# Evaluating all 16384 experts of the last block with matrix products from streamed tables, in place of gathering each token's 128 rows

## The chip, the cores and the metric

One core of a Trainium2 chip runs the whole program. A core has five engines that run side by side and meet only at semaphores: TensorE (matmul), VectorE, ScalarE, GpSimd, and SyncE, which here only issues DMAs. The metric is device microseconds of one execution, the median of the runs.

## The reference, cut to what matters

256 tokens of width 1024 pass two blocks (gated recurrence, latent attention, memory attention) and a last block of another kind: modulated norm, dilated attention beside a pooling mixer, and then a feed-forward part that picks experts. All is float32. The last part, for h = the normed and modulated tokens:

```
q = (h @ w_q).reshape(C, 8, 2, 128)                 # 8 retrieval heads, 2 halves
s = einsum('chpk,pnk->chpn', q, sub_keys)           # 128 sub-keys per half
sv, si = top_k(s, 16)
cand = sv[:,:,0,:,None] + sv[:,:,1,None,:]          # 256 candidates a head
top_v, top_pos = top_k(cand, 16)
eid = take(si0 * 128 + si1, top_pos)                # 16384 experts
gate = softmax(top_v)
act = gelu(einsum('cd,chkd->chk', h, expert_u[eid]))
y = einsum('chk,chkd->cd', gate * act, expert_v[eid])
out = rmsnorm(x + g2 * y, final_g)
```

Every token picks 8 x 16 = 128 of 16384 experts; an expert is one row of 1024 in each of two tables of 64 MB.

## The kernel before, in words

The program is unrolled. An order of tasks is written out for each engine and each of the three blocks: PE_ORDER, ACT_ORDER and ACT_LAST, DVE_ORDER and DVE_LAST; every engine works through its list strictly in order, and waits on semaphores inside a task. Tokens are two tiles of 128 (`t` and `u` in the names of tasks: K0at is unit K0, first half of its columns, tile 0). Weights come through `ring`, three slots of 2 MB, issued by SyncE; a slot is loaded again when TensorE has counted `unit_done`. Unit K2 alone goes to two other tiles (`aside`).

In the last block TensorE makes, after attention, the output product (tasks O1, O0), the transposes of the normed tokens into `xT` (Zt, Zu), the expert queries (K0 to K3, `expert_queries`) and the scores against the sub-keys (E0t to E3t, EU0, EU1, E4 to E7). VectorE turns scores into picks: `route(t, e)` is one top-16 search of a head and tile (tasks Rt0 to Rt7, Ru0 to Ru7), `experts_of` with `centre` finds the expert's numbers of a part of a tile (XP1 to XP7), and `gates_of` (GT) makes the gates, behind an exponential on ScalarE (T). OM, NM and Zu on VectorE are the residual sum, the norm and half of the scaling of the transposed tokens.

The picks are then gathered: for each of 256 pairs (tile, pick) GpSimd issues an indirect DMA (L626) that brings for each of 128 tokens a row of 8 KB, u and v of its expert side by side, into one of 15 slots. VectorE makes the dot product with the token (`dots_of`, L1841), ScalarE its gelu, times the gate, spread over a diagonal of 128x128 (`expert_weights`, L1305 to L1313), and TensorE sums diagonal x v rows into PSUM (L1087, tasks W). A slot is free again after that. The first gather is issued as soon as one head of tile 0 is known (XP1). At the end `end_sums` and `finish` add to x, norm and scale (FS, FN).

Before that, GpSimd multiplies the modulation matrix (L590 to L593) and mixes the pool. PSUM has two double tiles `pj` for units and outputs, and four banks that take turns (`bank_index`); from Zt on only two turn, since the others hold the sums. `do(...)` waits for its own instruction before the next one of the engine is issued.

Of the kernel before, what the change touches and what calls it, by code (L numbers as in the profile page):

```python
# [10 lines left out]


# [26 lines left out]
ROWS = PICKS * TT  # L39
GROUP = 4  # L40
N_SLOTS = 15
N_DIAG = 8
# [24 lines left out]
            Y5 O1u Zt O0v K0at E0t O0w K0bt E1t K1at Zu K1bt E2t K0au W4 K0bu E3t W5 W7 EU0 K1au W11 K1bu W15 EU1 W21  # L67
            K20 W27 K21 W31 K22 W32 K23 W36 E4 W37 E5 W40 K30 W42 K31 W45 K32 W49 K33 W55 E6 E7 W256"""]
# [4 lines left out]
ACT_LAST = """Xu BU BK BQa BQb SK S0 S1 MT S2 BV P0 P1 S3 S4 P2 S5 P3 P4 P5 OMt Zt K0at E0t T1 K0bt E1t OMu Zu K1bt W1  # L73
    E2t W5 E3t W7 K0bu W8 T2 W11 EU0 W18 K1bu W20 T3 W21 EU1 W35 K23 W38 E4 W39 E5 W51 T4 W57 K33 W61 E6 W62
    E7 W65 T5 W96 T6 W129 T7 W148 FN0 W256 FN1"""
# [4 lines left out]
DVE_LAST = """Xu S0 S1 S2 PL0 PL1 N0 N1 S3 N2 S4 S5 N3 N4 Y1 N5 OMt Y5 NMt Zt Rt0 XP1 OMu H2t NMu D1 Zu D3 H2u D4 GT1  # L80
    D5 Rt1 D8 XP2 D9 Rt2 D15 Rt3 D16 GT2 D18 XP3 D37 GT3 D44 Rt4 D50 Rt5 D54 XP4 D62 GT4 D63 Rt6 Rt7 D72 XP5
    D77 GT5 Ru0 D81 Ru1 D83 Ru2 Ru3 D89 XP6 D104 GT6 D105 Ru4 D106 Ru5 D110 Ru6 D115 Ru7 D121 XP7 D137 GT7
    D140 FS0 D156 FN0 D256 FS1 FN1"""


def pe_tasks():

    out, loads, pieces = [], 0, 0
    for text in PE_ORDER:
        tasks = []  # L90
        for task in text.split():
            if task == "LD":
                task, loads = f"LD{loads}", loads + 1
            if task == "AD":
                task, pieces = f"AD{pieces}", pieces + 1
            tasks.append(task)
        out.append(tasks)
    assert loads == pieces == N_MOD_PIECES
    return out
# [46 lines left out]
def big_uses():  # L146

    out, uses, turn = {}, [0, 0], 0
    for l, name in STREAM:
# [4 lines left out]
        elif name in ONE_SLOT or name == "C":  # L154
            if name in ("K1", "K2", "K3"):
                turn = 1
            out[l, name] = (turn, uses[turn])
            uses[turn] += 1
            turn = 1 - turn
    return out  # L160


BIG = big_uses()
# [12 lines left out]
def bank_uses(l, task):  # L176
# [7 lines left out]
    if task[0] == "E":  # L184
        return [(task,)]
# [21 lines left out]
EXPERT_PARTS = [(0, 0, 1), (0, 1, 2), (0, 2, 4), (0, 4, 6), (0, 6, 8), (1, 0, 4), (1, 4, 8)]  # L207


def part_starts():  # L210

    return {tile * PICKS + first * TOPK: n + 1 for n, (tile, first, last) in enumerate(EXPERT_PARTS)}


def bank_index():

    out, n, uses = {}, 0, [0, 0, 0, 0]

    def use(key, at):
        out[key] = (n, at, uses[at])  # L220
        uses[at] += 1
    for l in range(DEPTH + 1):
        few = False
        for task in TASKS[l]:
            few = few or (l == B2 and task == "Zt")
            for key in bank_uses(l, task):
                use((l, key), n % 2 if few else n % 4)
                n += 1
    return out, uses


def picks_order():

    free, out, last = [], [], {}
    for n in range(ROWS):
        if n in NEW_SLOTS:
            free = list(NEW_SLOTS[n][1]) + free
        k = free.pop(0)
        out.append((k, last.get(k), sum(1 for q in out if q[0] == k)))
        last[k] = n  # L240
        free.append(k)
    return out


NEW_SLOTS = {0: ("", range(0, 7)), 18: ("K1", (7, 8)), 41: ("K2", (9, 10)), 67: ("K3", (11, 12, 13)), 74: ("E7", (14,))}


def constants():
# [18 lines left out]
    for d in (4, 16):  # L267
# [14 lines left out]
        "c_iota": np.arange(16, dtype=np.float32).reshape(1, 16),  # L282
# [3 lines left out]
def build(nc, d, out):  # L286
# [8 lines left out]
    BANK, BANK_USES = bank_index()  # L295
    PICK = picks_order()

    with ExitStack() as ctx:
        def sb(name, shape, dt=f32):
            return ctx.enter_context(nc.sbuf_tensor(name, shape, dt))  # L300


# [8 lines left out]
        more_rows = sb("more_rows", [P, 2, D_MODEL])  # L311
# [4 lines left out]
        rope = sb("rope", [P, 2, T])  # L316
# [16 lines left out]
        qM = sb("qM", [P, MLA_HEADS, T])
        kM = sb("kM", [P, MLA_HEADS, T])
        vM = sb("vM", [P, TT, MLA_HEADS * MLA_V])
        qvE = sb("qvE", [P, 2, MEM_HEADS * T])
        qE = qvE[:, 0, :].rearrange("p (h t) -> p h t", t=T)
        kE = sb("kE", [P, MEM_HEADS, T])
        vE = qvE[:, 1, :].rearrange("p (a n) -> p a n", a=TT)
        sm = sb("sm", [P, 2, TT, T])  # L340
        pT = sb("pT", [P, 2, TT, T])
# [10 lines left out]
        w_pool, iota = flat_pair[:, 0:4 * P].rearrange("p (h t) -> p h t", t=P), mod_part[:, 1, 0:TOPK]  # L352
        sub_rows = flat_pair[:, 528:528 + 2 * P]
        row_gate1, row_scale2 = hv[:, 0, :], hv[:, 1, :]
        row_shift2, row_gate2, final_g = big[:, 0, :], big[:, 1, :], big[:, 2, :]
# [15 lines left out]
        def flat(tile):  # L371
# [15 lines left out]
        id_a, id_b = flat(vM)[:, 2 * PICKS:3 * PICKS], flat(vM)[:, 3 * PICKS:4 * PICKS]  # L387
        expert = flat(vM)[:, 512:768].bitcast(u32).rearrange("p (t j) -> p t j", t=TT)
        dots = flat(vM)[:, 768:1024].rearrange("p (t j) -> p t j", t=TT)
        onehot = flat(qT).rearrange("p (j i) -> p j i", i=TOPK)  # L390

        ring_rows = [[ring[:, UNIT[B2, unit] % RING, g * 2 * D_MODEL:(g + 1) * 2 * D_MODEL] for g in range(2)]
                     for unit in ("K1", "K2", "K3")]
        flat_y = flat(yT)
        aside = [flat(b), flat_y[:, 2 * D_MODEL:]]
        row_slot = ([flat(more_rows), flat(kM), flat(qvE), flat(qM)] + ring_rows[1] + [flat(hv)]
                    + ring_rows[0] + aside + ring_rows[2] + [flat(xT), flat_y[:, 0:2 * D_MODEL]])
        assert len(row_slot) == N_SLOTS
        diag = [far_pair[:, g, :] for g in range(4)] + [causal[:, g // 2, (g % 2) * P:(g % 2 + 1) * P] for g in range(4)]
        assert len(diag) == N_DIAG  # L400
        junk = [flat_pair, big[:, 0, :]]
        acts, weights_of = rope[:, 0, :], rope[:, 1, :]
        first_scores = [sm[:, i // 2, i % 2, :] for i in range(4)] + [pT[:, i // 2, i % 2, :] for i in range(4)]
        later_scores = kT
        pj = [ctx.enter_context(nc.psum_tensor(f"pj{i}", [P, 1024], f32)) for i in range(2)]
# [46 lines left out]
        SCORES_OF = {name: n for n, name in enumerate(t for t in ACT_LAST.split() if t[0] == "E")}  # L452
# [29 lines left out]
        N_B2 = 5  # L482
# [5 lines left out]
        def _(sp):  # L488
# [5 lines left out]
            def weights(n):  # L494

                if STREAM[n] == (B2, "K2"):
                    sp.wait_ge(sem("pool_out"), 2)
                    for g in range(2):
                        load(aside[g], d["units"][n, :, g * 2 * D_MODEL:(g + 1) * 2 * D_MODEL], "aside_load")
                    return  # L500
# [31 lines left out]
            for l in range(DEPTH + 1):  # L532
                units = [name for k, name in LOADS if k == l]
                for name in units:
# [14 lines left out]
                    if UNIT[l, name] > 1 and name != "K2":  # L549
                        weights(UNIT[l, name])  # L550
                    if name == "K0":
                        weights(UNIT[l, "K2"])
                    if name == units[3] and l == B2:
# [4 lines left out]
                        for row, c in ((row_gate1, 2), (row_scale2, 4), (row_shift2, 3), (row_gate2, 5)):  # L558
                            load(row, mod_rows[c * DC:(c + 1) * DC, :].rearrange("(o c) p -> o (c p)", o=1)
# [1454 lines left out]
```

## Time and profile before

| | |
|---|---|
| time, median of 3 runs | 1456.43 us (1456.28 to 1457.4) |
| span of the profiled execution | 1455.4 us |
| TensorE busy | 1312.6 us (90%) |
| VectorE busy | 815.5 us (56%) |
| GpSimd busy | 647.9 us (45%) |
| ScalarE busy | 412.4 us (28%) |
| moved by DMA | 407.7 MB, mean 280 GB/s |

The shares of busy time are means over parts with different limits, so they must be read by stretch. Matmuls are pipelined, and a busy TensorE is not one at its peak.

### The profile page before, as it was taken

What the parts mean: (1) busy time and instruction counts of PE and PEld (TensorE: products, weight loads), DVE (VectorE), ACT (ScalarE), POOL (GpSimd) and SP (SyncE); (2) the same over time, 40 slices, a digit from 0 to 9 for tenths busy, and PEclk for the clock granted to TensorE, in tenths of its full rate; (3) what the DMA queues carried; (4) which work ended last, traced back from release to release, by engine and by line L of the source; (5) the groups of instructions that cost most, each with busy time, mean ns of one, the idle gap of its engine ahead of it and who ended that gap; (6) DMA issues with size and microseconds to landing.
All of it is one profiled execution on the core that took longest, in us unless ns stands there. A gap on an engine that the chain in (4) does not pass through costs nothing.

```text
span 1455.4 us, 14776 instructions
## 1 busy us (share of the span) xinstructions
PE 1312.6 (90%) x4936; PEld 829.2 (57%) x4936; DVE 815.5 (56%) x1680; ACT 412.4 (28%) x1032; POOL 647.9 (45%) x643
## 2 busy tenths in 40 slices
PE   9999999999999999999998989967877787778886
PEld 8888687747888687747656646533333332323332
DVE  0775377431465367443237775879887654544555
ACT  0532244211332244112232332322313232122123
POOL 0556667331546667331202434454544454544440
PEclk9999999999999999999999999988989899999999
DMA  9544334345443334357255999999999999999995
GB/s 375 189 160 174 116 152 172 133 184 199 187 161 158 132 143 176 116 202 257 69 231 232 377 413 409 421 420 419 420 419 421 419 420 420 420 420 420 420 420 211
DMA packets 53734, 407.71 MB, mean 280 GB/s; under 512 B 6150, under 2 KB 8731, under 8 KB 11035
## 3 DMA queue, kind: packets, MB, share of 16 engines
q0 software_dynamic: 36864, 268.45, 44.7%
q1 hardware_dynamic: 15706, 137.28, 24.2%
q10 hardware_dynamic: 1088, 1.05, 0.4%
q8 instruction: 39, 0.64, 0.2%
q14 instruction: 37, 0.30, 0.1%
HBM read 404.63 MB, written 1.07 MB: 279 GB/s over the span
## 4 chain that ended last, share of the span: by engine, by line
PE 63%; DMA 23%; DVE 7%; issue 3%; ACT 2%; POOL 1%; ACTq 0%; POOLq 0%; DVEq 0%
PE pj L665 23%; DMA ring<-in_peer_uv,vM 10%; PE bank L1087 10%; PE pj L701 9%; PE pj L680 7%; DMA yT<-in_peer_uv,vM 5%; PE bank L805 3%; DMA more_rows<-in_peer_uv,vM 3%; DMA qvE<-in_peer_uv,vM 2%; PE pj L957 2%; DMA hv<-in_peer_uv,vM 2%; DMA qM<-in_peer_uv,vM 1%; PE bank L638 1%; PE bank L907 1%; DVE tri L1841 1%
## 5 line engine op out<-in xcount | busy, mean ns | idle before, releaser
L665 PE MATMUL pj<-xT,ring 128*128 128x256 f32 (+2 forms) x1536 | 324.3, 371 | 1.8 <-ACTq L1135 1.7
L665 PEld LDWEIGHTS pj<-xT,ring 128*128 128x128 f32 (+1 forms) x1536 | 277.7, 189 | 42.4 <-issue 2.7
L592 POOL TENSOR_SCALAR more_rows<-more_rows,lbt 128x256 f32<-128x256 f32 x168 | 178.4, 1062 | 16.4
L626 POOL DMA_INDIRECT ring<-in_peer_uv,vM x101 | 120.1, 1189 | 116.5 <-PE bank L1087 104.4
L590 POOL TENSOR_SCALAR mod_part<-more_rows,lbt 128x256 f32<-128x256 f32 x24 | 26.1, 1088 | 271.2 <-issue 120.0
L701 PE MATMUL pj<-ring,yT 128*128 128x512 f32 x320 | 140.3, 594 | 0.0
L1305 ACT ACTIVATE rope<-vM 128x4 f32<-128x4 f32 (+3 forms) x84 | 17.1, 204 | 408.0 <-DVE big L1841 325.2
L593 POOL TENSOR_TENSOR mod_part<-mod_part,more_rows 128x256 f32<-128x256 f32 x168 | 126.5, 753 | 14.0
L1087 PE MATMUL bank<-ring,causal 128*128 128x512 f32 x200 | 99.3, 635 | 17.4 <-ACT causal L1313 17.4
L1087 PE MATMUL bank<-ring,tri 128*128 128x512 f32 x204 | 97.6, 618 | 16.5 <-ACT tri L1313 16.5
L701 PEld LDWEIGHTS pj<-ring,yT 128*128 128x128 f32 x320 | 59.9, 190 | 71.1 <-issue 71.1
L1841 DVE SCALAR_TENSOR_TENSOR big<-ring,memT 128x1024 f32<-128x1024 f32 x51 | 62.7, 1230 | 48.3 <-DMA ring<-in_peer_uv,vM 48.1
L1841 DVE SCALAR_TENSOR_TENSOR tri<-ring,memT 128x1024 f32<-128x1024 f32 x50 | 61.3, 1226 | 48.2 <-DMA ring<-in_peer_uv,vM 48.1
L1087 PEld LDWEIGHTS bank<-ring,causal 128*128 128x128 f32 x200 | 39.6, 202 | 70.4 <-issue 45.3
L1087 PEld LDWEIGHTS bank<-ring,tri 128*128 128x128 f32 x204 | 39.8, 199 | 69.5 <-issue 46.4
L626 POOL DMA_INDIRECT more_rows<-in_peer_uv,vM x20 | 21.7, 1087 | 121.9 <-DVE vM L1811 79.4
L680 PE MATMUL pj<-ring,xT 128*128 128x512 f32 x160 | 70.3, 594 | 0.0
L805 PEld LDWEIGHTS bank<-big 128*128 128x128 f32 x480 | 57.4, 192 | 3.9 <-issue 3.2
L805 PE MATMUL bank<-big 128*128 128x128 f32 x480 | 58.4, 275 | 0.0
L1307 ACT ACTIVATE rope<-rope,rstd 128x1 f32<-128x1 f32 x256 | 56.6, 284 | 2.8
L680 PEld LDWEIGHTS pj<-ring,xT 128*128 128x128 f32 x160 | 29.9, 190 | 34.6 <-issue 34.4
L957 PEld LDWEIGHTS pj<-xT,ring 128*128 128x128 f32 x320 | 43.3, 199 | 6.2 <-issue 4.7
(366 smaller groups left out, 2146.3 us busy)
## 6 DMA issues: line engine op xcount, KB each, us to landing
ring<-in_units SPq DMA_DIRECT2D x44, 2048.0 KB, 9.3
more_rows<-in_w_ada SPq DMA_DIRECT2D x24, 1024.0 KB, 4.8
ring<-in_units SPq DMA_DIRECT2D x2, 1536.0 KB, 6.5
ring<-in_peer_uv,vM POOLq DMA_INDIRECT x101, 23.2
memT<-in_mem SPq DMA_DIRECT2D x1, 1024.0 KB, 5.4
ring<-in_units SPq DMA_DIRECT2D x2, 512.0 KB, 6.6
ring<-in_units SPq DMA_DIRECT2D x1, 1024.0 KB, 9.0
xT<-in_x_turned SPq DMA_DIRECT2D x1, 1024.0 KB, 10.8
```

Of the source, the lines that this page charges most:

```text
L590: do(g.tensor_scalar(part, mod_w[:, 0, :], silu_c[:, 0:1], None, ALU.mult))
L592: do(g.tensor_scalar(mod_w[:, c, :], mod_w[:, c, :], silu_c[:, c:c + 1], None, ALU.mult))
L593: do(g.tensor_tensor(part, part, mod_w[:, c, :], ALU.add), "mod_partial" if c == DC - 1 else None)
L626: pool.indirect_dma_start(row_slot[k], None, d["peer_uv_2"], bass.IndirectOffsetOnAxis(ap=expert[:, t, j:j + 1], axis=0))\
L665: ins = nc.tensor.matmul(pj[s][0:n, 2 * m + first:2 * m + stop], ring[:, slot, at:at + n], act[:, c, first:stop], start=(c == 0), stop=(c ...
L680: ins = nc.tensor.matmul(pj[s][:, t * COLS:(t + 1) * COLS], act[:, c, t * P:(t + 1) * P], w[:, c, :], start=(c == 0), stop=(c == DC - 1))
L701: ins = nc.tensor.matmul(pj[t][:, n * 512:(n + 1) * 512], yT[:, 4 * j + c, t * P:(t + 1) * P], w[:, c, n * 512:(n + 1) * 512], start=(firs ...
L805: ins = nc.tensor.matmul(B[:, n * P:(n + 1) * P], k, q, start=True, stop=True)
L957: ins = nc.tensor.matmul(pj[s][:, 2 * m * P + first:2 * m * P + stop], w[c][:, m * P:(m + 1) * P], xT[:, c, first:stop], start=(c == 0), s ...
L1087: ins = nc.tensor.matmul(bank[2 * (1 - t) + half][:, :], diag[n % N_DIAG], row_slot[PICK[n][0]][:, c0:c0 + COLS], start=(j == 0), stop=(j ...
L1307: a.activation(weights_of[:, n0 + k:n0 + k + 1], acts[:, n0 + k:n0 + k + 1], ACT.Copy, scale=gate[:, t, j + k:j + k + 1]).then_inc(sem("ro ...
L1841: v.scalar_tensor_tensor(out=junk[0 if one else n % 2], in0=row_slot[k][:, 0:D_MODEL], scalar=1.0, in1=normed[:, t, :], op0=ALU.mult, op1= ...
```

## The change

In the last block all experts are evaluated for all tokens. `expert_units` lays the two tables out as 64 + 64 pieces of 1 MB, each a pair of first-key values with all 128 second keys (256 experts); SyncE streams them through four half slots of the ring. Task u`p` (of 64) makes u x tokens for pair p, ScalarE's Gelu puts it into `mixture`, 128 second keys x (128 first keys x 256 tokens). The gates are spread over it by one-hot products: for a group of four tokens (tasks g0 to g63) a one-hot of the first keys (`left`, built by GpSimd for three groups of four, else by VectorE) times a one-hot of the second keys scaled by the gates (`right`, VectorE) gives 128 x 128 gates a token, with which VectorE multiplies the columns of `mixture` that are there (`group_weighted`); for pairs that come later ScalarE stores the gates first and VectorE multiplies them by the pair's Gelu (`pair_weighted`). Groups run between pairs 34 and 63. The first keys, second keys and gates of a tile are turned by TensorE before (it0 after u17, it1 after u33). Then tasks v0 to v63 sum mixture x v into `pj`. The gather, the dots, the diagonals and their products go. Expert numbers are no longer put together; the four parts of picks have four heads each. K2 goes through the ring. The banks turn by four throughout. Most tiles of the earlier blocks lie now inside one arena with `mixture`.

```diff
-            Y5 O1u Zt O0v K0at E0t O0w K0bt E1t K1at Zu K1bt E2t K0au W4 K0bu E3t W5 W7 EU0 K1au W11 K1bu W15 EU1 W21
-            K20 W27 K21 W31 K22 W32 K23 W36 E4 W37 E5 W40 K30 W42 K31 W45 K32 W49 K33 W55 E6 E7 W256"""]
+            Y5 O1u Zt O0v K0at O0w K0bt E0t K1at E1t K1bt E2t E3t Zu K0au K0bu K1au EU0 K1bu K20 EU1 K21 K22 K23 K30
+            E4 E5 K31 K32 K33"""]
...
-DVE_LAST = """Xu S0 S1 S2 PL0 PL1 N0 N1 S3 N2 S4 S5 N3 N4 Y1 N5 OMt Y5 NMt Zt Rt0 XP1 OMu H2t NMu D1 Zu D3 H2u D4 GT1
...
+DVE_LAST = """Xu S0 S1 S2 PL0 PL1 N0 N1 S3 N2 S4 S5 N3 N4 Y1 N5 OMt Y5 NMt Zt Rt0 OMu NMu Rt1 Zu Rt2 Rt3 XP1 Rt4
+    Rt5 GT1 Rt6 Rt7 XP2 Ru0 Ru1 GT2 Ru2 Ru3 XP3 Ru4 Ru5 GT3 Ru6 Ru7 XP4 GT4"""
+N_PAIRS = 64
+N_GROUPS = 64
+LEAD = 3
+def expert_tasks():
+
+    out = ["u0", "E6", "E7"]
+    for p in range(1, N_PAIRS):
+        if p > FIRST_MIXED:
+            share = N_GROUPS * (p - FIRST_MIXED) // (N_PAIRS - 1 - FIRST_MIXED)
+            before = N_GROUPS * (p - 1 - FIRST_MIXED) // (N_PAIRS - 1 - FIRST_MIXED)
+            out += [f"g{g}" for g in range(before, share)]
+        out.append(f"u{p}")
+        if p in TURNED_AFTER:
+            out.append(f"it{TURNED_AFTER.index(p)}")
+    return out + [f"v{p}" for p in range(N_PAIRS)]
+TURNED_AFTER = (17, 33)
+FIRST_MIXED = 34
+LEFT_BY_POOL = [g for g in range(N_GROUPS) if g % 4 != 3]
+EXP_AFTER = {1: 1, 9: 2, 21: 3, 31: 4}
...
+            for n in range(2 * N_PAIRS):
+                if n < 4:
+                    unit_done(sp, B2, ("K1", "K1", "K2", "K2")[n])
+                elif n - 4 < N_PAIRS:
+                    bank_filled(sp, (B2, (f"u{n - 4}",)))
+                else:
+                    sp.wait_ge(sem("values_summed"), n - 4 - N_PAIRS + 1)
+                load(pieces[n % 4], d["experts"][n], f"piece_load{n % 4}")
...
+            unit_done(pool, B2, "K3")
+            for g in LEFT_BY_POOL:
+                pool.wait_ge(sem("picks_turned"), 4 * g // P + 1)
+                if g >= LEAD:
+                    bank_filled(pool, (B2, (f"g{g - LEAD}",)))
+                for k in range(4):
+                    t = 4 * g + k
+                    g_left = left[g % LEAD][:, k, :]
+                    nc.gpsimd.tensor_scalar(g_left, iota, first_turned[:, t:t + 1], None, ALU.is_equal)\
+                        .then_inc(sem("left_built"), 1)
...
+                elif task[0] == "u":
+                    p = int(task[1:])
+                    key = (l, (task,))
+                    pe.wait_ge(sem(f"piece_load{p % 4}"), 16 * (p // 4 + 1))
+                    bank_empty(pe, key)
+                    for k in range(2):
+                        for c in range(DC):
+                            at = (k * DC + c) * P
+                            ins = nc.tensor.matmul(bank_of(key)[:, k * T:(k + 1) * T], pieces[p % 4][:, at:at + P],
+                                                   xT[:, c, :], start=(c == 0), stop=(c == DC - 1))
+                    last(ins)
+                elif task[0] == "g":
...
+                    for k in range(4):
+                        ins = nc.tensor.matmul(bank_of(key)[:, k * P:(k + 1) * P], left[g % LEAD][:, k, :],
+                                               right[g % LEAD][:, k, :], start=True, stop=True)
+                    last(ins)
+                elif task[0] == "v" and int(task[1:]) < N_PAIRS - 2:
...
+                    for k in range(2):
+                        for t in range(TT):
+                            for half in range(2):
+                                at = k * D_MODEL + half * COLS
+                                ins = nc.tensor.matmul(pj[t][:, half * COLS:(half + 1) * COLS],
+                                                       mixture[:, 2 * p + k, t * P:(t + 1) * P],
+                                                       pieces[n % 4][:, at:at + COLS],
+                                                       start=(p == 0 and k == 0), stop=False)
+                    last(ins, "values_summed")
...
+                    if known:
+                        turn = p - FIRST_MIXED - 1
+                        if turn >= 2:
+                            act.wait_ge(sem("pair_weighted"), turn - 1)
+                        if known < T:
+                            do(a.activation(mixture[:, e, known:T], B[:, :, known:T], ACT.Gelu))
+                        do(a.activation(hidden_of[p % 2][:, :, 0:known], B[:, :, 0:known], ACT.Gelu), *bank_free(key))
+                    else:
+                        do(a.activation(mixture[:, e, :], B, ACT.Gelu), *bank_free(key))
+                    act.sem_inc(sem("hidden"), 1)
+                    if p in EXP_AFTER:
+                        top_exp(EXP_AFTER[p])
...
+            def right_of(g):
...
+                if g not in LEFT_BY_POOL:
+                    t = 4 * g
+                    v.tensor_tensor(left[g % LEAD], iota.unsqueeze(1).to_broadcast([P, 4, P]),
+                                    first_turned[:, t:t + 4].unsqueeze(2).to_broadcast([P, 4, P]),
+                                    ALU.is_equal).then_inc(sem("left_filled"), 1)
+                for k in range(4):
+                    t = 4 * g + k
+                    v.tensor_scalar(right[g % LEAD][:, k, :], iota, second_turned[:, t:t + 1], gate_turned[:, t:t + 1],
+                                    ALU.is_equal, ALU.mult).then_inc(sem("right_built"), 1)
+
+            def group_weighted(g):
...
+                do(v.tensor_tensor(part, bank_of(key)[:, :].rearrange("p (t e) -> p e t", t=4)[:, 0:e, :], part, ALU.mult),
+                   *bank_free(key))
...
+            def pair_weighted(p):
...
+                do(v.tensor_tensor(part, hidden_of[p % 2][:, :, 0:known], part, ALU.mult), "pair_weighted")
```

## Rows read from the trace of the kernel before

**Rows 1.** The page's slices: clock and DMA in 40 equal parts of the span.
```profile
PEclk9999999999999999999999999988989899999999
DMA  9544334345443334357255999999999999999995
```

**Rows 2.** Busy time by stretch, two stretches; the first line names the columns.
```profile
core 0: us, PE busy (x) PEld busy (x) DVE busy (x) ACT busy (x) POOL busy (x), PEclk, DMA share, GB/s
8.00:35.00 27.00, 27.00 (x126) 22.39 (x125) 0.00 (x0) 1.01 (x1) 0.00 (x0) 1.00 1.00 406
900.00:1400.00 500.00, 397.11 (x891) 174.92 (x890) 329.37 (x778) 131.99 (x481) 240.44 (x204) 0.92 1.01 420
```

**Rows 3.** The page's DMA queues: packets, MB, share of the engines; the gather's queue.
```profile
q0 software_dynamic: 36864, 268.45, 44.7%
```

**Rows 4.** The chain that ended last: start, length in us, what; around 1200 us.
```profile
1184.74 3.46 PE bank L1087 x4
...
1188.46 23.30 DMA ring<-in_peer_uv,vM
```

**Rows 5.** Timeline: start, length in us, engine and line; transposes, one search, OMu, norm.
```profile
761.57 1.04 PE L638 MATMUL bank<-eye,memT 128*128 128x128 f32 x8
...
771.38 0.49 DVE L1754 MAX8 cT<-sm 128x8 f32<-128x128 f32 x2 [6.92 <-ACTq L1413]
...
775.56 0.42 DVE L1782 FIND_INDEX8 kE<-rstd,sq 128x8 uint32<-128x256 f32 x1
...
781.76 0.69 DVE L1926 TENSOR_TENSOR x<-x,tri 128x512 f32<-128x512 f32 x1
...
785.90 0.75 DVE L1533 TENSOR_SCALAR memT<-x,stat 128x1024 f32<-128x1024 f32 x1
```

**Rows 6.** DMA issues: operation, count, KB each, median us from issue to landing.
```profile
more_rows<-in_w_ada SPq DMA_DIRECT2D x24, 1024.0 KB, 4.8
...
yT<-in_units SPq DMA_DIRECT2D x1, 1024.0 KB, 18.7
```

**Rows 7.** The chain that ended last, as above: runs of matmuls of each form.
```profile
113.27 1.78 PE bank L805 x16
115.06 6.91 PE pj L665 x32
...
270.45 13.84 PE pj L701 x32
...
766.04 3.59 PE pj L957 x32
```

**Rows 8.** Timeline of the end: the last four matmuls.
```profile
1445.41 1.98 PE L1087 MATMUL bank<-ring,causal 128*128 128x512 f32 x4 [0.50 <-ACT causal L1313]
```

**Rows 9.** Groups of VectorE from 700 us on, by form: busy us, mean ns of one.
```profile
L1772 DVE TENSOR_TENSOR sq<-cT 128x256 f32<-128x256 f32 x16 | 6.5, 406 | 0.0
L1801 DVE TENSOR_TENSOR qT<-mod_part,vM 128x1024 f32<-128x1024 f32 x4 | 4.7, 1221 | 0.0
...
L1853 DVE TENSOR_TENSOR pT<-bank,big 128x512 f32<-128x512 f32 x4 | 2.8, 690 | 2.3 <-PE bank L1087 2.3
```

**Rows 10.** Groups of ScalarE from 700 us on, the same columns: the table loads.
```profile
L1305 ACT ACT_TABLE_LOAD x8 | 10.3, 1283 | 20.5 <-DVE big L1841 11.7 <-DVE tri L1841 8.6 <-ACT yT L1386 0.2
```

**Rows 11.** Groups of GpSimd; the last row: one line's durations, min/median/max in ns.
```profile
L592 POOL TENSOR_SCALAR more_rows<-more_rows,lbt 128x256 f32<-128x256 f32 x168 | 178.4, 1062 | 16.4
...
L602 POOL COPY b<-kT 128x256 f32<-128x256 f32 x10 | 4.0, 398 | 0.6
...
L597 POOL COPY kT<-kT 128x1024 f32<-128x1024 f32 x1 | 1.0, 1035 | 50.2 <-ACTq L1348 50.2
...
L592 POOL TENSOR_SCALAR more_rows<-more_rows,lbt x168: 924/926/1777, 47.6 to 631.3; 128x256 f32<-128x256 f32 x168
```

**Rows 12.** VectorE's tensor_scalar on two lines: min/median/max in ns.
```profile
L1479 DVE TENSOR_SCALAR sm<-sm x4: 293/294/453, 54.1 to 385.4; 128x256 f32<-128x256 f32 x4
...
L1533 DVE TENSOR_SCALAR memT<-x,stat x4: 752/753/754, 656.1 to 785.9; 128x1024 f32<-128x1024 f32 x4
```

More of the change, by code:

```diff
@@ L13 @@
+import math
 import numpy as np
@@ L72 @@
     Le18 HO2 HN2 HO3 HN3 LN"""
-ACT_LAST = """Xu BU BK BQa BQb SK S0 S1 MT S2 BV P0 P1 S3 S4 P2 S5 P3 P4 P5 OMt Zt K0at E0t T1 K0bt E1t OMu Zu K1bt W1
-    E2t W5 E3t W7 K0bu W8 T2 W11 EU0 W18 K1bu W20 T3 W21 EU1 W35 K23 W38 E4 W39 E5 W51 T4 W57 K33 W61 E6 W62
-    E7 W65 T5 W96 T6 W129 T7 W148 FN0 W256 FN1"""
+ACT_LAST = """Xu BU BK BQa BQb SK S0 S1 MT S2 BV P0 P1 S3 S4 P2 S5 P3 P4 P5 OMt Zt K0at K0bt E0t OMu K1bt E1t E2t E3t Zu
+    K0bu EU0 K1bu EU1 K23 E4 E5 K33"""
 DVE_ORDER = """F0 N FP0 R0 R1 R2 R3 Da01 KR Da02 S0 Db01 P0 Db02 L01 Da03 S1 L02 AD Db03 Da04 F1 AD S2 Da05 L03 Da06
@@ L159, in big_uses @@
             turn = 1 - turn
-    return out
-BIG = big_uses()
+    return out, uses
+BIG, BIG_USES = big_uses()
 N_MLA = 6
@@ L394, in build @@
[L394 to L401, printed above, removed]
@@ L402, in build @@
-        acts, weights_of = rope[:, 0, :], rope[:, 1, :]
         first_scores = [sm[:, i // 2, i % 2, :] for i in range(4)] + [pT[:, i // 2, i % 2, :] for i in range(4)]
         later_scores = kT
+        mixture = arena[:, :].rearrange("p (e t) -> p e t", t=T)
+        piece_at = [(UNIT[B2, unit] % RING, half) for unit in ("K1", "K2") for half in range(2)]
+        pieces = [ring[:, slot, half * 2 * D_MODEL:(half + 1) * 2 * D_MODEL] for slot, half in piece_at]
+        spare = ring[:, UNIT[B2, "K3"] % RING, :]
@@ new lines, in build @@
+        left = [spare[:, k * 512:(k + 1) * 512].rearrange("p (t i) -> p t i", t=4) for k in range(LEAD)]
+        right = [spare[:, 512 * (LEAD + k):512 * (LEAD + k + 1)].rearrange("p (t i) -> p t i", t=4) for k in range(LEAD)]
+        hidden_of = [spare[:, 512 * (2 * LEAD + k):512 * (2 * LEAD + k + 1)].rearrange("p (e t) -> p e t", e=2)
+                     for k in range(2)]
+        row_gate2, final_g = spare[:, 0:D_MODEL], spare[:, D_MODEL:2 * D_MODEL]
+        ends = [spare[:, k * COLS:(k + 1) * COLS] for k in range(4, 6)]
@@ L943, in expert_queries @@
             def expert_queries(name, columns, tiles):
-                if name == "K2":
-                    pe.wait_ge(sem("aside_load"), 32)
-                    w = [rows.rearrange("p (c n) -> p c n", c=DC // 2)[:, c, :] for rows in aside for c in range(DC // 2)]
-                else:
-                    slot = loaded(l, name)
-                    w = [ring[:, slot, c * COLS:(c + 1) * COLS] for c in range(DC)]
+                slot = loaded(l, name)
+                w = [ring[:, slot, c * COLS:(c + 1) * COLS] for c in range(DC)]
                 s, use = BIG[l, name]
@@ L1423, in _ @@
+            log_exp_tables()
+            for t in range(TT):
+                half_norm(t, "x_last", squares)
         @block.vector
@@ L1807, in experts_of @@
                 for k, (op, arg, place, found) in enumerate(half_ids):
-                    do(v.tensor_reduce(found[:, 0:n], ohs[k], X, ALU.add), behind=1 - k)
-                do(v.scalar_tensor_tensor(out=id_a[:, 0:n], in0=id_a[:, 0:n], scalar=float(NKEYS), in1=id_b[:, 0:n],
-                                          op0=ALU.mult, op1=ALU.add))
-                do(v.tensor_copy(expert[:, t, js], id_a[:, 0:n]), "experts")
+                    do(v.tensor_reduce(found, ohs[k], X, ALU.add), behind=1 - k)
             def centre(part):
@@ L1863, in finish @@
                     c = slice(half * COLS, (half + 1) * COLS)
-                    do(v.tensor_scalar(x[:, t, c], pT_of[half], stat[:, 12 + t:13 + t], None, ALU.mult), "result")
-            dots_first = [task[1:] for task in DVE_LAST.split("H2u")[0].split() if task[0] == "D"]
-            SAME_JUNK = max([4] + [int(n) for n in dots_first])
-            used = 0
+                    do(v.tensor_scalar(x[:, t, c], ends[half], stat[:, 12 + t:13 + t], None, ALU.mult), "result")
             for task in DVE_LAST.split():
```

341 lines of the change are left out of this document (166 added, 175 removed).

## The prediction, made before the changed kernel ran

> **What bounds the kernel now.** I read the profile in this order: the page's slices, the busy time and bytes per stretch, the chain that ended last, then rows of single operations. The slices show TensorE's granted clock at or near its upper level (2.4 GHz) and the DMA engines about half used until a little past the middle, then DMA full for everything that follows [rows 1]. From 900 to 1400 us the 16 DMA engines are busy all the time and move 420 GB/s, while TensorE is busy 397 us of 500, VectorE 329 and GpSimd 240 [rows 2]. What they move is the software queue's 268.45 MB, the gathered expert rows: 256 picks x 128 tokens x 8 KB [rows 3]. 268.45 MB at 420 GB/s is 639 us, by far the longest thing after 800 us. The chain of waits says the same: in it a few microseconds of matmuls stand between one landing of over 20 us and the next [rows 4]. So the last 600 us are bound by bytes gathered. The part before 762 us is bound by TensorE, and the change leaves it alone (one table instead of two and three broadcast rows fewer are loaded there, hidden behind matmuls; I take nothing).
>
> **The change, part by part.** It removes the gather, the dot products, the 128x128 diagonals and their 1024 products, and puts in three dense parts on TensorE. I follow TensorE from the transposes of tile 0, which stand at 761.57 us [rows 5], to the end, since every new part passes through it.
>
> *Bytes.* The tables are 16384 x 1024 x 4 B twice, 134.2 MB, half of what was gathered: 320 us at 420 GB/s. Each pair's matmuls below take 3.46 us for a piece of 1.05 MB, which asks for 303 GB/s. At the kernel's start TensorE ran without a gap while DMA moved 406 GB/s [rows 2], so both at once is possible. A piece is issued when the pair four before it is done, so it has three pair times, 10.4 us, to land; a 1 MB load in rows of 8 KB landed in 4.8 us [rows 6]. DMA is then hidden.
>
> *Queries and scores to the first pair.* Half a query unit of one tile is 32 products of 128 columns, 3.59 us [rows 7]. From 761.57: transposes 1.0, O0v 3.5, K0at 3.6, O0w 3.5, K0bt 3.6, score E0t 0.7, that is 777.5. VectorE's first search (Rt0) so starts at 778.0, after the copy; a search takes 4.6 us, from 771.38 to 775.98 in the trace [rows 5]. Then OMu, four operations of 0.69 with gaps, ends at 785.5. The norm of tile 1 ended 786.65 - 782.45 = 4.2 us after OMu [rows 5], of which about 1 us was other VectorE work now removed: 788.7. VectorE now places Rt1 (4.6) ahead of its half of Zu (1.75): 795.1. TensorE meanwhile runs K1at, K1bt and the scores to 788 and has nothing to do until 795; here the order costs it some 6 us. Then K0au, K0bu, K1au, K1bu 14.4; K20 to K33 eight times 1.73 = 13.8; EU0, EU1, E4, E5 about 3.7: the first pair starts at 827.
>
> *Pairs (u).* 64 x 16 = 1024 products of 128x256. Thirty-two of them took 6.91 us with their weight loads hidden, 0.216 each [rows 7]: 221 us. E6, E7 and the two turns of the picks add 2.5.
>
> *Groups (g).* 64 x 4 products of 128 columns at 1.78/16 = 0.111 [rows 7]: 28.5 us.
>
> *Values (v).* 64 x 8 = 512 products of 128x512 at 13.84/32 = 0.4325 [rows 7]: 221.4 us. Since they follow the last pair and piece loads are four ahead, I see no gap at the joint; the weighting of the last group hides under pair 63.
>
> *End.* After the last product VectorE still has the first tile's scaling to finish (its sums became available only 3.4 us earlier), so the second tile's four operations of 0.69 start about 1.2 us late. 1.2 + 2.9 + 1.4 (products with the final gain) + 0.8 (refining) + 1.0 (scaling) + 2.2 (store and close) = 9.5 us. Before, the span ended 8.0 us after its last product at 1447.4 [rows 8].
>
> TensorE's floor: 827 + 221 + 2.5 + 28.5 + 221.4 + 9.5 = 1310 us of span.
>
> *Are the picks there in time?* VectorE has 16 searches of 4.6 and four expert parts of four heads: six operations of 128x1024 at 1.22 [rows 9] and small ones, 9.2. Rt2, Rt3, XP1 end at 813.5; E4 comes at 822.5, Rt4, Rt5 end at 831.7; GT1 waits for the exponential behind pair 1 (838); Rt6, Rt7, XP2, Ru0, Ru1, GT2 end at 867, while TensorE asks for them after pair 17, at 891. Ru2 to Ru5 and XP3 end at 894, GT3 waits for the exponential behind pair 21 (907), Ru6, Ru7, XP4 end at 926, GT4 waits for pair 31 (942), and TensorE asks after pair 33, at 947. So slacks of 24 and 5 us: no cost, though the second is thin. ScalarE's two table loads of 1.28 [rows 10] around each exponential are covered by four banks of 3.46 us.
>
> *Mixed part: the term in doubt.* Groups run between pairs 34 and 63. TensorE needs 29 x 3.46 + 28.5 = 129 us there. In the same time:
> GpSimd builds the left one-hots of 48 groups: 192 scalar comparisons of 128x128. No such operation is in the trace. Its nearest is the 128x256 multiplication, 0.926 median when undisturbed, 1.062 in the mean [rows 11]. Copies of 256 and 1024 cost 0.398 and 1.035, so 0.83 ns an element and 0.186 fixed. If all but 0.186 of the 0.926 grows with the length, 128 columns cost 0.186 + 0.37 = 0.56; if only the copy's slope does, 0.926 - 0.106 = 0.82. The outer ends are 0.56 and, with nothing saved by shortness and the mean's disturbance, 1.06. I take the midpoint 0.69 times 1.062/0.926 = 1.15, thus 0.79, because VectorE will be busier beside it than it was then. Three groups are built ahead, 180 remain: 142 us.
> VectorE: a right one-hot is a tensor_scalar of 128x128; 0.294 at 256 and 0.753 at 1024 [rows 12] give 0.218. Four are 0.87. Weighting a group reads 394 elements in the mean from PSUM (8 x the pairs ahead); 0.406 at 256 and 0.690 at 512 [rows 9] give 0.56. 64 x 1.43 + 16 left one-hots x 0.69 + 29 pairs x 0.41 + gaps 4 = 118 us; with the 15% of disturbance 136. That the access is strided is not in the trace; it may cost nothing or double the 64 x 0.41 us of elements, + 26.
> GpSimd thus sets the pace by a little, with VectorE close behind, and with only three buffers of one-hots two engines at 90% don't overlap perfectly: I add 6 us. 148 in place of 129: + 19.
> The Trainium skill bears on this (GPSIMD Engine Reference, section 3.1): a one-input body costs about 1.03 cycles an element, however simple. The copies' 0.83 ns agree [rows 11]; by it the comparison would lie at the 0.82 end, times 1.15 = 0.94, and the part would be 180 x 0.94 + 6 = 175, + 46 in place of + 19. That result is one of the rivals.
> Its section 8 says GpSimd shares its SBUF interfaces with VectorE when that works with two SBUF inputs or in its two-port mode; by that the four right one-hots would slow GpSimd most, which no row here can single out.
>
> *Sum.* 1310 + 19 = 1329 us of span. The profiled execution has a span of 1455.4 against the median of 1456.43, so 1 us lies around it: 1330 us.
>
> **Rivals.**
> 1. *TensorE alone bounds.* GpSimd's comparison costs 0.56 to 0.65: 180 x 0.65 = 117, under 129. Time 1310 + 1 + a few of coupling = 1313. For it: the short row. Against it: its mean is 15% over its median already with VectorE half busy.
> 2. *The mixed part is much longer.* GpSimd at 0.94 to 1.06, 175 to 197 us, or VectorE with doubled strided access, 118 + 26 = 144, x 1.15 = 166. Time 1357 to 1379. TensorE idles a quarter of such a part, and where it idled a fifth of the time, the granted clock was 0.92 in the mean, so at the lower level (1.2 GHz) for some of it [rows 2], which adds little as it isn't what is waited for.
> 3. *Late pieces: slower than before.* If a piece lands in L, four pieces in flight let a pair pass every L/3. From L = 10.4 us on this is the bound; at L = 13.6 (128 x (4.53 - 3.46) = 137 us) all gain is gone. A 1 MB load in the trace did take 18.7 us [rows 6], which would make 128 x 6.2 = 798 us of the two dense parts, some 1690 us in all. Against it: that load shared the engines with the gather, and 4.8 us is the figure without.
> 4. *The change doesn't do what it says*: the picks come late and TensorE waits before the groups as it now waits for rows. VectorE's second chain has 5 us of slack; 15% on its last 50 us is 8, less 5, and a start of VectorE 10 us later would add as much: 1335 to 1345.
>
> **How the numbers follow.** Forecast (1320 to 1348) 0.47; rival 1 (1305 to 1320) 0.22; rival 2 0.16; rival 4 0.07; rival 3 0.04; an unseen cost of either kind that leaves it still faster 0.04. The range reaches down to rival 1 and up to most of rival 2: 1305 to 1378, which leaves out about 0.12 to 0.2. Slower by over 0.2% are rival 3 beyond L = 13.6 and unseen mechanisms: 0.05. Within 0.2% (3 us, what a measurement of this kernel can tell from no change): 0.01. Faster: 0.94.
>
> **What would show it.** Right: DMA at about 300 GB/s with a busy share near 0.7 from 827 us on; pairs 3.46 us apart at granted clock 1.0; the first pair at 827 and the first value product near 1098; TensorE in the mixed part waiting for GpSimd's one-hots, and none of them in the value part, which takes 221 us. Rival 1: no wait of TensorE in the mixed part. Rival 2: GpSimd's comparison at 0.9 us or more, or VectorE's weighting over 0.8. Rival 3: TensorE waiting for the ring's pieces. Rival 4: TensorE idle before the turn of the picks, released by the VectorE step that makes the gates. The prediction is wrong if the dense products don't hold their 0.216 and 0.4325 beside streaming.

## The result: 1801 us, slower by 24%, and the profile after

The changed kernel takes 1800.97 us (1800.11 to 1802.15) against 1456.36 us before, a ratio of 1.236 (95% interval 1.2345 to 1.238). The prediction said 1330, in 1305 to 1378. Not only the size is wrong but the sign.

The busy time by stretch of the kernel after: the pairs alone, the part where groups are mixed in, and the value part. The columns are those of [rows 2].

```profile
850.00:1090.00 240.00, 240.00 (x1124) 211.46 (x1123) 75.64 (x313) 37.00 (x58) 7.00 (x12) 1.00 0.42 146
1090.00:1348.00 258.00, 258.00 (x1445) 233.96 (x1444) 128.81 (x352) 38.62 (x121) 111.43 (x180) 1.00 0.35 122
1352.00:1790.00 438.00, 438.00 (x1023) 194.06 (x1022) 6.57 (x13) 4.12 (x9) 0.00 (x0) 1.00 0.43 149
```

TensorE is busy in every microsecond of all three, at granted clock 1.00 (2.4 GHz). DMA, which was full and moved 420 GB/s in [rows 2], now moves 122 to 149 GB/s at a busy share of 0.35 to 0.43. The bound has moved from the bytes to TensorE, as intended, but TensorE has more to do than DMA had.

How much more, the groups of the kernel after say (line, shape and count, then busy us and mean ns of one):

```profile
L1096 PE MATMUL bank<-xT,ring 128*128 128x256 f32 x2048 | 447.5, 379 | 0.0
L1128 PE MATMUL pj<-ring,arena 128*128 128x512 f32 x992 | 425.9, 592 | 0.0
...
L1109 PE MATMUL bank<-ring 128*128 128x128 f32 x512 | 61.8, 275 | 0.0
```

The code of L1096 issues 64 x 16 = 1024 products; the trace has 2048 records. L1128 issues 62 x 8 = 496, the trace has 992 (L1142 has the last 16 as 32); L1109 issues 256, the trace 512. Each record lasts what the prediction took for a whole product: 447.5/2048 = 0.218, 425.9/992 = 0.429, 61.8/512 = 0.121. **A float32 product stands in the trace as two matmul records, and the prediction multiplied the number of products in the code by the time of one record.**

The chain that ended last, for the same stretch (start, length, what), is matmuls almost alone:

```profile
859.52 117.42 PE bank L1096 x544
977.27 110.51 PE bank L1096 x512
...
1352.48 425.73 PE pj L1128 x992
1778.21 13.75 PE pj L1142 x32
```

| stretch | predicted | measured |
|---|---|---|
| to the first pair | 827 | 850.7 |
| pairs and groups | 271 | 501.6 |
| values | 221.4 | 439.7 |
| after the last product | 9.5 | 7.5 |
| span | 1329 | 1799.5 |

The measured ones go by the starts 850.7 (first L1096 matmul) and 1352.3 (first L1128 one), and the end at 1778.21 + 13.75 = 1792.0. The sum with two records a product, 2048 x 0.216 + 512 x 0.111 + 2.5 = 502 and 1024 x 0.4325 = 443, gives both dense parts to 1%. Every duration in it was in the trace before [rows 7].

### The profile page after: what moved, and what is told of

It is laid out like the page before. It is cut to its first block, busy times and chain, and to the rows that moved or that the text cites. A ratio compares the mean times of both kernels' runs of the same rounds, so it can differ in the third digit from the quotient of the medians.

```text
span 1799.5 us, 19294 instructions
## 1 busy us (share of the span) xinstructions
PE 1766.4 (98%) x7502; PEld 1267.8 (70%) x7502; DVE 622.3 (35%) x1467; ACT 316.3 (18%) x589; POOL 464.8 (26%) x579
## 4 chain that ended last, share of the span: by engine, by line
PE 97%; DVE 1%; ACT 1%; issue 1%; DMA 0%; ACTq 0%; SPq 0%; DVEq 0%
PE bank L1096 25%; PE pj L1128 24%; PE pj L675 19%; PE pj L711 8%; PE pj L690 5%; PE pj L963 3%; PE bank L1109 3%; PE bank L815 3%; PE bank L648 1%; PE bank L917 1%; PE pj L1142 1%; PE bank L776 1%; PE bank L849 0%; PE bank L831 0%; PE bank L795 0%
## 5 line engine op out<-in xcount | busy, mean ns | idle before, releaser
L1096 PE MATMUL bank<-xT,ring 128*128 128x256 f32 x2048 | 447.5, 379 | 0.0
L1128 PE MATMUL pj<-ring,arena 128*128 128x512 f32 x992 | 425.9, 592 | 0.0
L1096 PEld LDWEIGHTS bank<-xT,ring 128*128 128x128 f32 x2048 | 386.7, 190 | 51.2
L1128 PEld LDWEIGHTS pj<-ring,arena 128*128 128x128 f32 x992 | 188.5, 190 | 236.8 <-issue 236.8
L637 POOL TENSOR_SCALAR ring<-near,causal 128x128 f32<-128x128 f32 x192 | 118.4, 634 | 518.3 <-ACTq L1460 277.5
L613 POOL TENSOR_SCALAR arena<-arena,lbt 128x256 f32<-128x256 f32 x168 | 176.1, 1048 | 16.4
L711 PE MATMUL pj<-ring,arena 128*128 128x512 f32 x320 | 140.3, 594 | 0.0
L614 POOL TENSOR_TENSOR mod_part<-mod_part,arena 128x256 f32<-128x256 f32 x168 | 128.3, 764 | 14.0
L711 PEld LDWEIGHTS pj<-ring,arena 128*128 128x128 f32 x320 | 59.9, 190 | 71.1 <-issue 71.1
L1911 DVE TENSOR_SCALAR ring<-near,causal,mod_part 128x128 f32<-128x128 f32 x256 | 76.6, 362 | 7.2 <-DVE arena L1922 1.8
L963 PE MATMUL pj<-xT,ring 128*128 128x128 f32 (+1 forms) x384 | 61.7, 325 | 12.7 <-issue 7.4
L1109 PEld LDWEIGHTS bank<-ring 128*128 128x128 f32 x512 | 61.7, 192 | 1.5
L1109 PE MATMUL bank<-ring 128*128 128x128 f32 x512 | 61.8, 275 | 0.0
```

The costliest lines, as they stand in the source:

```text
L613: do(g.tensor_scalar(mod_w[:, c, :], mod_w[:, c, :], silu_c[:, c:c + 1], None, ALU.mult))
L614: do(g.tensor_tensor(part, part, mod_w[:, c, :], ALU.add), "mod_partial" if c == DC - 1 else None)
L637: nc.gpsimd.tensor_scalar(g_left, iota, first_turned[:, t:t + 1], None, ALU.is_equal)\
L711: ins = nc.tensor.matmul(pj[t][:, n * 512:(n + 1) * 512], yT[:, 4 * j + c, t * P:(t + 1) * P], w[:, c, n * 512:(n + 1) * 512], start=(firs ...
L963: ins = nc.tensor.matmul(pj[s][:, 2 * m * P + first:2 * m * P + stop], w[c][:, m * P:(m + 1) * P], xT[:, c, first:stop], start=(c == 0), s ...
L1096: ins = nc.tensor.matmul(bank_of(key)[:, k * T:(k + 1) * T], pieces[p % 4][:, at:at + P], xT[:, c, :], start=(c == 0), stop=(c == DC - 1))
```

## The experiments

Theory A: a float32 product takes two records, so TensorE alone sets the time. Theory B: a product takes what was predicted, and streaming stretches it, by late pieces or contention. That 2048 records are there speaks for A; the first two experiments test it from either side. Runs e1, e2 and e4 leave work out or use wrong weights, so they are tests and not kernels to use.

**e1_v_half** sums only the first 128 experts of each pair:

```diff
-                    for k in range(2):
+                    for k in range(1):
                         for t in range(TT):
                             for half in range(2):
                                 at = k * D_MODEL + half * COLS
```

> Leaves out half of the sum over experts: of each pair only the first 128 experts are summed into the output, 256 fewer products of 128x512; everything else is as in the changed kernel, all 128 pieces are still loaded. Theory A (each float32 product stands in the trace as two matmul records of 0.43 us, so it takes 0.865 us, twice what the prediction counted): the value part shrinks by 248 x 0.865 = 214.5 us (pairs 62 and 63 keep theirs), 1801 becomes 1586. Theory B (a product takes 0.43 us as predicted and the value part is stretched by late pieces or by contention with their streaming): the part stays at about 440 us or loses at most 107 us, so 1694 to 1801.

Measured 1589.66 us, 211.3 less than 1800.97. The value products of this kernel:

```profile
L1128 PE MATMUL pj<-ring,arena 128*128 128x512 f32 x496 | 213.0, 592 | 0.0
```

and its value part, columns as in [rows 2]:

```profile
1350.00:1580.00 230.00, 229.79 (x542) 102.65 (x540) 8.05 (x16) 4.74 (x11) 0.00 (x0) 1.00 0.82 285
```

248 products fewer are 496 records and 213 us fewer: 0.86 us each. DMA now moves 285 GB/s and TensorE is still busy 229.8 of 230 us, so the pieces are not late even at nearly twice the rate. This is theory A, 4 us above its 1586.

**e2_stream_once** loads four pieces in all:

```diff
-                load(pieces[n % 4], d["experts"][n], f"piece_load{n % 4}")
+                if n < 4:
+                    load(pieces[n % 4], d["experts"][n], f"piece_load{n % 4}")
...
-                    pe.wait_ge(sem(f"piece_load{p % 4}"), 16 * (p // 4 + 1))
+                    pe.wait_ge(sem(f"piece_load{p % 4}"), 16)
```

> Leaves the streaming out: only the first four pieces are loaded, all pairs use them again, so the products are the same in number and form but most have the wrong weights. Theory A (TensorE's own count of passes): within 3 us of the changed kernel, 1798 to 1804, with DMA near zero in the dense parts. Theory B (streaming stretches the products): towards the predicted 1330, at least 100 us less than 1801.

Measured 1801.11 us, 0.1 more. Busy time by stretch of this kernel, columns as in [rows 2]: DMA moves 1 GB/s or less.

```profile
1200.00:1350.00 150.00, 150.00 (x844) 136.11 (x843) 78.48 (x204) 21.37 (x72) 64.99 (x104) 1.00 0.00 1
1350.00:1580.00 230.00, 230.00 (x545) 103.12 (x544) 0.69 (x1) 1.88 (x2) 0.00 (x0) 1.00 0.00 0
```

Streaming 134 MB costs this kernel nothing; theory B falls. At the pace that the prediction had in mind, about 300 GB/s, the bytes are tested by e4.

**e3_left_all_pool** gives all left one-hots to GpSimd:

```diff
-LEFT_BY_POOL = [g for g in range(N_GROUPS) if g % 4 != 3]
+LEFT_BY_POOL = [g for g in range(N_GROUPS)]
```

> GpSimd builds the left one-hots of all 64 groups instead of 48. It costs 0.634 us each in the changed kernel's trace: 256 x 0.634 = 162 us of GpSimd in a mixed part that TensorE fills for 257 us. Theory A (TensorE bounds the mixed part, with slack of about 95 us for GpSimd): no change, 1799 to 1803. Rival (the prediction's: the builders set the pace of the mixed part): longer by up to 64 x 0.634 = 41 us.

Measured 1800.87 us: no change. In a stretch of its mixed part (columns as in [rows 2]) GpSimd is busy 86 us of 150, in place of 65 in the same stretch of e2, which has the split of the changed kernel, and TensorE all of it:

```profile
1200.00:1350.00 150.00, 150.00 (x843) 136.11 (x843) 74.20 (x195) 21.37 (x72) 85.91 (x140) 1.00 0.35 120
```

The builders don't set the pace at TensorE's true speed.

**e4_both_half** asks what the rest of the prediction was worth: it gives TensorE, in the pairs and in the values, the work that the prediction had counted. The one-hot products of the groups stay as they are, so they still cost twice what was counted. It is e1 and, for the pairs:

```diff
-                        for c in range(DC):
+                        for c in range(DC // 2):
                             at = (k * DC + c) * P
...
-                                                   xT[:, c, :], start=(c == 0), stop=(c == DC - 1))
+                                                   xT[:, c, :], start=(c == 0), stop=(c == DC // 2 - 1))
```

> Leaves out half of the sum over experts and half of the sum over channels in the expert products: 512 fewer products of 128x256 and 248 fewer of 128x512, so TensorE has in both dense parts about what the prediction gave it. Theory A: 1801 - 512 x 0.432 - 248 x 0.865 = 1801 - 221 - 214.5 = 1365 us if TensorE still bounds the mixed part (29 pairs x 3.46 + 64 groups x 0.89 = 157 us there; GpSimd 192 x 0.634 = 122, VectorE about 64 x 1.8 + 30 = 145). If the builders bound it, some 5 to 20 us more, 1370 to 1385. Pieces then have to come at 303 GB/s. Theory B (streaming is the limit): pieces are waited for, above 1450.

Measured 1368.11 us, 3 from theory A's 1365. The mixed part of this kernel and a stretch of its value part:

```profile
970.00:1130.00 160.00, 160.00 (x991) 147.77 (x991) 128.01 (x356) 39.94 (x126) 112.43 (x180) 1.00 0.58 202
...
1200.00:1350.00 150.00, 150.00 (x350) 66.32 (x350) 0.88 (x2) 0.00 (x0) 0.00 (x0) 1.00 0.85 299
```

and the one-hot products of its groups:

```profile
L1109 PE MATMUL bank<-ring 128*128 128x128 f32 x512 | 61.8, 275 | 0.0
```

So with half the dense products the change would have been faster than before by 6.1% (ratio 0.939, 0.9365 to 0.942). Pieces at 299 GB/s, the pace of the prediction, are never late. In the mixed part TensorE is busy all 160 us, VectorE 128 and GpSimd 112, so TensorE bounds it here too. But TensorE has some 157 us of work there, because of the 512 records of the groups; the prediction had given it 129, and VectorE's 128 us would be level with that. Which of the two would then set the pace is not shown by any run.

**e5_norm_first** mends the order that cost TensorE two idle times ahead of the first pair. In the kernel after, the chain shows them: 7.4 us before 785.04, and VectorE's search and scaling before 803.38. The first costs more than its length: K1at behind it takes 6.13 us at a mean granted clock of 0.60, so for most of it at the lower level (1.2 GHz), where K1bt of the same form takes 3.59 at 1.00.

```profile
777.18 0.45 PE bank L973 x4
777.63 7.41 issue
785.04 6.13 PE pj L963 x32
791.17 0.45 PE bank L973 x4
791.62 3.59 PE pj L963 x32
...
803.22 0.03 DVEq L1611
803.25 0.14 issue
803.38 12.67 PE pj L963 x96
```

```diff
-DVE_LAST = """... Zt Rt0 OMu NMu Rt1 Zu Rt2 Rt3 ...
+DVE_LAST = """... Zt OMu NMu Zu Rt0 Rt1 Rt2 Rt3 ...
```

> Only VectorE's order changes: the residual sum, the norm and the scaling of tile 1 stand ahead of the searches Rt0 and Rt1. In the changed kernel's trace TensorE idles 7.4 us before 785 us (K1at waits for the output tile that OMu frees, which stands behind Rt0) and about 8 us before 803 us (K0au waits for VectorE's half of Zu, behind Rt1). Theory: both idle times go, 12 to 15 us less, 1786 to 1789. Rival: the searches moved back make the picks late for the groups: then the time comes back before the groups; but TensorE now asks for them some 100 us later than predicted, so no.

Measured 1787.59 us, 13.4 less. In the same chain of this kernel the first gap is gone (7.4 us), K1at (776.70) takes 3.57 us (2.6 less), and K0au starts at 789.23; the wait for VectorE's scaling before it is 2.1 us in place of 5.3 (3.3 less), so a little of the second idle time stays:

```profile
772.69 3.57 PE pj L963 x32
776.70 3.57 PE pj L963 x32
780.72 3.59 PE pj L963 x32
...
789.23 12.58 PE pj L963 x96
```

**e6_half_words** changes what bounds: the dense products alone in bfloat16, so the output's precision is another. The tables are converted by the loads themselves, which GpSimd now issues into eight half-size buffers. The order of e5 is kept, and all left one-hots are VectorE's.

```diff
+        half_words = mybir.dt.bfloat16
+        mixture = arena[:, 0:N_PAIRS * T].bitcast(half_words).rearrange("p (e t) -> p e t", t=T)
+        xT_half = arena[:, 82 * T:86 * T].bitcast(half_words).rearrange("p (c t) -> p c t", t=T)
...
+            do(nc.gpsimd.tensor_copy(xT_half, xT[:, :, :]), "xT_half_ready")
+            for n in range(2 * N_PAIRS):
...
+                nc.gpsimd.dma_start(pieces[n % 8], d["experts"][n]).then_inc(sem(f"piece_load{n % 8}"), 16)
...
-LEFT_BY_POOL = [g for g in range(N_GROUPS) if g % 4 != 3]
+LEFT_BY_POOL = []
```

> The dense products alone in bfloat16: pieces are converted by the GpSimd queue's DMAs on their way into 8 half-size buffers, the tokens by one GpSimd copy, the mixture is kept in bfloat16; queries, scores, picks and gates stay float32; VectorE builds all left one-hots; the order of norm first. It changes the precision of the expert products. Theory A (a float32 product is two records because of its type, a bfloat16 one is a single record of half the length or so, 0.107 us for 256 columns): both dense parts leave TensorE's bound and become DMA's or VectorE's: 835 + pairs at 2.5 us to 34, then VectorE with 64 x (0.35 x 4 + 0.56 + 0.72) + 12 = 183 us, then 64 pieces at 2.5 us: 1240 to 1330 in all. Rival (the record's length is set by columns and weight loads of 128x128 whatever the type): records stay at 0.216 and 0.43 us, one each, so the parts halve: 1801 - 15 - 443 = 1343 or more.

Measured 1248.77 us, 208 us or 14% less than before (ratio 0.8577, 0.8562 to 0.8591); e5's order, worth 13.4 us in the float32 kernel, is part of that. Groups of this kernel, columns as above:

```profile
L1091 PE MATMUL bank<-arena,ring 128*128 128x256 bf16 x1024 | 124.7, 281 | 7.1 <-ACT arena L1470 4.2 <-DMA ring<-in_experts 2.7
L1123 PE MATMUL pj<-ring,arena 128*128 128x512 bf16 x486 | 114.1, 378 | 30.2 <-DMA ring<-in_experts 29.4 <-DVEq L1919 0.5
...
L1104 PE MATMUL bank<-ring 128*128 128x128 f32 x512 | 70.9, 283 | 41.7 <-DVE ring L1906 41.7
```

The 1024 products of the pairs are now 1024 records of 0.122 us, and the values' 496 are 486 in the trace (a few records are missing) of 0.235. The one-hot products, still float32, are still 512 for 256. So the pairs of records belong to the type. Each bfloat16 record is also only a little over half of a float32 record, so a product falls to 0.28 of its float32 time.

What binds there, by stretch of the same kernel: in the mixed part (the first two lines) VectorE, for whose one-hots TensorE waits 41.7 us, and in the value part DMA.

```profile
950.00:1000.00 50.00, 36.99 (x313) 33.37 (x311) 46.67 (x132) 12.61 (x38) 4.77 (x9) 1.00 0.58 99
1000.00:1080.00 80.00, 55.95 (x455) 50.15 (x456) 75.14 (x195) 17.04 (x58) 7.42 (x14) 0.98 0.55 93
1100.00:1200.00 100.00, 76.13 (x321) 29.11 (x327) 0.00 (x0) 0.00 (x0) 22.02 (x42) 1.00 1.06 214
```

**e8_gather_half_words** is the control: the kernel before with the expert rows and the diagonals in bfloat16, gather and all.

```diff
+        row_slot = [rows[:, 0:D_MODEL].bitcast(mybir.dt.bfloat16) for rows in row_slot]
+        diag = [square[:, 0:P // 2].bitcast(mybir.dt.bfloat16) for square in diag]
```

> The kernel before, with the same lower precision in the same place: the gathered rows are converted to bfloat16 by their DMA, the diagonals are bfloat16, so a product of the gather's sum is one bfloat16 record instead of two float32 ones. It asks whether the gain of the half-word version comes from the type alone. Theory (the gather is bound by the bytes that DMA reads, 268 MB at 420 GB/s): the bytes read stay, so 1450 to 1460, although TensorE's work for the picks falls from 440 us to about 120. Rival (the type is what brings it, or DMA is bound by the bytes written): at least 100 us less, near 1150 if written bytes count.

Measured 1440.06 us against 1457.15 beside it (ratio 0.9888, 0.9871 to 0.9904): 17 us less, 10 under the lower end expected. Its busy time, columns as in [rows 2]:

```profile
900.00:1400.00 500.00, 189.67 (x490) 68.29 (x490) 334.00 (x788) 133.09 (x489) 226.24 (x206) 0.61 1.06 214
```

TensorE's busy time falls from 397 to 190 us and the DMA engines stay full. (All 512 products of the picks have 512 records here, where the kernel before has 1024. They are busy 211 us and not the expected 120, at a granted clock of 0.61 in this stretch; this costs nothing, as they are not the bound.) The 214 GB/s count the half-size words written; read from memory are twice that, 428 GB/s, where it was 420. So the bytes written are not what bounds the gather. The bytes read and the number of rows are both as before, and this run can't tell one from the other. The type alone gives 1.1 of the 14 per cent. Of the 17 us, 268.45 MB at 428 in place of 420 are 12; where the other 5 come from is open.

**e9_half_words_left** lets GpSimd build every second left one-hot between its DMA issues. The edit is shown against e6.

```diff
-LEFT_BY_POOL = []
+LEFT_BY_POOL = [g for g in range(N_GROUPS) if g % 2 == 1]
...
+                elif int(task[1:]) + LEAD < N_GROUPS:
+                    left_of(int(task[1:]) + LEAD)
```

> The half-word dense version, with every second group's left one-hot built by GpSimd between its DMA issues instead of by VectorE. In the half-word version VectorE is busy 0.9 of the mixed part and TensorE waits for its one-hots. Theory (VectorE bounds the mixed part): 32 x 0.69 = 22 us less of VectorE, some of it lost to slower VectorE operations beside GpSimd: 1228 to 1242 against 1249. Rival (GpSimd's builds of 4 x 0.634 us hold back the issue of pieces or take the place of VectorE as the bound): 1245 or more.

Measured 1238.85 us (1235.54 to 1239.71), 10 less than e6 and 15% less than before (ratio 0.8507, 0.8493 to 0.8521). This lies in the theory's range, with about half of the 22 us of VectorE's relief. TensorE still waits 27.2 us for the right one-hots, in place of 41.7; where the rest of the relief went is not shown. By stretch:

```profile
950.00:1000.00 50.00, 40.74 (x345) 36.79 (x343) 46.26 (x132) 13.86 (x42) 37.22 (x56) 1.00 0.65 111
1000.00:1080.00 80.00, 64.31 (x490) 53.12 (x488) 65.57 (x170) 17.77 (x57) 49.63 (x74) 0.98 0.65 114
```

It is the fastest version here, at a lower precision of the expert products than either kernel.

## Why the prediction was wrong, point by point

**The step that failed: the cost of a product.** Under "Pairs", "Groups" and "Values" the counts 1024, 256 and 512 are right, and so are the durations 0.216, 0.111 and 0.4325; their product is not. The durations came from the chain's rows as length over the "x" of the row [rows 7], and that x counts records. The runs show two records for each float32 product (2048 for 1024, 512 for 256), so 0.43, 0.22 and 0.86 us a product. The rows could have been held against the code. K0at is two columns of eight products, 16, and its row says x32: the prediction even wrote "32 products" for it. The page of before shows 320 records at the output product's line for (4 + 4 + 2) units x 16 = 160 products:

```profile
L701 PE MATMUL pj<-ring,yT 128*128 128x512 f32 x320 | 140.3, 594 | 0.0
```

The prediction also gave the removed products by the trace's number ("their 1024 products" for 256 picks x 2 halves = 512) and the new ones by the code's, and did not ask why such numbers differ. The three terms were 221, 28.5 and 221.4; by records the first two are 442 and 57, which with the 2.5 for E6, E7 and the turns fill the measured 501.6 us, and the values measured 440. That is + 468 us. The start with + 24, the end with - 2 and the mixed part's - 19 nearly cancel, which leaves the miss of 471.

By the right count the sum was decided in the first lines: 442 + 57 + 443 = 942 us of TensorE in place of 639 us of gathering.

**The start.** Predicted 827, measured 850.7. 13.8 us are the same mistake in the eight whole columns of K2 and K3. About 8 us are a wait that the prediction overlooked: it let K1at run behind E0t, but K1at writes the output tile that OMu frees, and OMu stands behind Rt0 on VectorE. It did find the second idle time, VectorE's half of Zu behind Rt1. e5 takes away the first and part of the second and gives 13.4 us, 2.6 of them because K1at no longer runs at the lower clock.

**The mixed part.** The term + 19 was zero, as the window and e3 show: TensorE's 258 us cover GpSimd's 111 and VectorE's 129. GpSimd's comparison of 128x128 was put between 0.56 and 1.06, with 0.79 taken after the disturbance; it measured 0.634. VectorE's right one-hot was put at 0.218 and measured 0.344. The weighting of a group measured 0.559 in the median (L1922), as the 0.56 that was taken, so its strided access cost nothing. These are the rows of the kernel after, first a group (busy us, mean ns), then one line's min/median/max in ns:

```profile
L637 POOL TENSOR_SCALAR ring<-near,causal 128x128 f32<-128x128 f32 x192 | 118.4, 634 | 518.3 <-ACTq L1460 277.5
...
L1911 DVE TENSOR_SCALAR ring<-near,causal,mod_part x256: 332/344/494, 1077.1 to 1340.0; 128x128 f32<-128x128 f32 x128
```

The two errors have opposite signs. So the engine that was to set the pace, GpSimd with 142 us, needed only 111, and VectorE's 129 would have equalled the 129 us predicted for TensorE. What the part would then have cost is open, since in e4 TensorE still had 157. Rival 2's time for slow VectorE was also summed wrong: 166 in place of 129 us is 1310 + 37 + 1 = 1348, and not 1357 or more.

**The Trainium skill's rule** on one-input bodies (GPSIMD Engine Reference, section 3.1, about 1.03 cycles an element) was weighed at 0.82 us. The trace disagrees: the comparison took 0.634, and 0.634 at 128 columns with 0.926 at 256 [rows 11] makes 2.3 ns an element (a rough slope, from a mean and a median of two different operations), although the copies with their 0.83 follow the rule.

**The bytes** were right. Pieces landed in 4.9 us, as the 4.8 of [rows 6]; DMA kept up with 285 GB/s in e1 and 299 in e4, and taking it away changed nothing (e2). **The picks' time** was not tested in the changed kernel, because TensorE asked for them far later than predicted. In e4, with pairs at the predicted pace but 25 us later, TensorE never waited for them. **The end** was 7.5 us for 9.5: I had the first tile's work delay the second by 1.2 us, but with its true speed TensorE gives VectorE 6.9 us between the tiles in place of 3.4.

**The rivals.** None was this. The one that ended slower, late pieces, was the wrong mechanism. The likeliest error of such a sum, a factor in the unit in which TensorE's time was counted, had no chance of its own. A change that puts 1792 products on TensorE in place of 512 in order to halve bytes should have had one.

## What to carry to other kernels

Before a duration per instruction is multiplied by a count from the code, divide the trace's count for a known line by the code's count for it; here the quotient was 2 for every float32 product, and for bfloat16 it was 1. When work moves from the DMA queue to an engine, first sum the new work on that engine alone: 942 us of dense float32 products against 639 us of gathered bytes says the sign before any overlap is thought about. What made the dense form pay was the type of its products, and the control (e8) shows that the type without the dense form gives only 1.1%.

## What the runs showed of the hardware beyond that

A load on GpSimd's queue that converts float32 to bfloat16 on its way read at about twice the 213 to 214 GB/s that it wrote: in e6 and in e8 the cost did not go by the bytes written. In both the rows read were of 8 KB, so a cost by bytes read and one by rows are not told apart. TensorE's granted clock was 0.61 in the mean over 500 us of e8, where TensorE was busy 38% of the time, thus at the lower level (1.2 GHz) for most of them; the DMA engines stayed full meanwhile.
